# Mixers of a hybrid decoder block: the output transposes and the attention copy take fixed places, and the diagonal products go ahead of the state product

## What is computed

```python
cb = jnp.einsum('bclgn,bcsgn->bcgls', Cc, Bc)
y_diag = jnp.einsum('bcgls,bgjcls,bcsgjp->bclgjp', cb, lmat, X)       # diagonal products
states = jnp.einsum('bclgn,bgjcl,bclgjp->bcgjpn', Bc, decay_states, X)  # state product
h = h * dc[..., None, None] + st                                       # state add, chunk by chunk
y_off = jnp.einsum('bclgn,bcgjpn,bgjcl->bclgjp', Cc, prev, jnp.exp(a_cs))
y = y_diag + y_off + D * xh
y = gated_group_rms_norm(y, z, ssd_norm_w)                             # y * silu(z), normalised per group
probs = softmax with sink over a window of 128 keys; out = probs @ v    # attention
```

## Time and profile before

| | |
|---|---|
| median of 3 runs (lowest to highest) | 2089.53 us (2088.35 to 2092.85) |
| the profiled execution: its time / its span | 2091.65 us / 2090.0 us |
| mean granted TensorE clock | 0.988 of full speed |
| TensorE busy | 2003.9 us, 96% of the span |
| VectorE busy | 1402.8 us, 67% |
| ScalarE busy | 991.1 us, 47% |
| GpSimd busy | 655.4 us, 31% |
| HBM traffic | 122 GB/s over the span |

### The profile page before, as it was taken

How to read it: one execution, slowest core, us unless ns; L and a number is a source line. 1 busy time by engine, 2 the same in 40 slices (tenths; PEclk the granted TensorE clock), 3 DMA queues, 4 the chain that set the end, 5 groups by cost and what they waited for, 6 DMA issues and landing times. The chain is left out here.

```text
span 2090.0 us, 26993 instructions
## 1 busy us (share of the span) xinstructions
PE 2003.9 (96%) x9516; PEld 1618.7 (77%) x9516; DVE 1402.8 (67%) x1892; ACT 991.1 (47%) x1847; POOL 655.4 (31%) x477
## 2 busy tenths in 40 slices
PE   6999999999999898989899999999999999999997
PEld 6787788888866666766578888888888888888886
DVE  6867776865768787878743444569877787753523
ACT  5543344444367666676642223445443444343532
POOL 6524334422365555556400000015222222100000
PEclk9999999999999999999999999999999999999999
DMA  4244324433354444344454443312222222455453
GB/s 156 91 115 138 127 88 152 146 106 114 126 190 132 137 117 148 118 140 117 159 172 168 141 148 125 123 73 85 81 75 90 90 72 78 157 175 189 117 147 92
DMA packets 166092, 261.99 MB, mean 125 GB/s; under 512 B 18400, under 2 KB 108896, under 8 KB 165984
## 3 DMA queue, kind: packets, MB, share of 16 engines
q1 hardware_dynamic: 132016, 217.06, 32.2%
q0 software_dynamic: 8368, 30.94, 4.3%
q10 hardware_dynamic: 25600, 12.59, 2.0%
HBM read 191.73 MB, written 63.57 MB: 122 GB/s over the span
## 5 line engine op out<-in xcount | busy, mean ns | idle before, releaser
L2736 DVE TENSOR_TENSOR lt_d_lo<-lt_w_raw,lt_d_hi 128x640 fp32r<-128x640 f32 (+1 forms) x62 | 55.2, 891 | 133.2 <-ACT lt_d_hi L2435 133.1
L163 PE MATMUL ps_zg<-z_w,u_hi 128*128 128x512 f32 x256 | 110.9, 433 | 0.5 <-POOL z_w L688 0.5
L2306 POOL TENSOR_TENSOR lt_t_f<-lt_w_raw 128x512 f32<-128x512 f32 x21 | 29.1, 1384 | 261.6 <-DVE lt_t_lo L2664 259.8
L994 DVE TENSOR_TENSOR fr_w_lo<-fr_w_f,fr_w_hi 128x512 fp32r<-128x512 f32 x72 | 57.1, 809 | 79.9 <-ACT fr_w_hi L754 61.0
L2435 ACT ACTIVATE lt_d_hi<-lt_w_raw 128x640 fp32r<-128x640 f32 (+1 forms) x62 | 49.1, 792 | 118.5 <-PE lt_ps L165 102.2
L1535 POOL TENSOR_TENSOR mx_seg<-mx_seg,mx_cbm 128x1024 f32<-128x1024 f32 x31 | 75.0, 2418 | 94.1 <-ACT mx_seg L1614 78.5
L165 PE MATMUL ps_zg<-z_w,u_lo 128*128 128x512 f32 x256 | 103.4, 404 | 0.0
L164 PE MATMUL ps_zg<-z_w,u_hi 128*128 128x512 f32 x256 | 102.8, 402 | 0.0
L2393 ACT ACTIVATE lt_t_hi<-lt_t_f 128x512 fp32r<-128x512 f32 x84 | 52.5, 628 | 100.1 <-PE lt_ps L165 61.9
L643 POOL TENSOR_TENSOR fr_w_f<-fr_raw_b 128x512 f32<-128x512 f32 x24 | 36.8, 1534 | 185.3 <-PE fr_ps_x L165 71.0
L2480 ACT ACTIVATE lt_w_hi<-lt_w_raw 128x1024 fp32r<-128x1024 f32 x22 | 23.2, 1060 | 147.4 <-PE lt_ps L165 147.4
(11 more groups left out here) (535 smaller groups left out, 6740.3 us busy)
## 6 DMA issues: line engine op xcount, KB each, us to landing
lt_w_raw<-in_w_up SPq DMA_DIRECT2D x44, 512.0 KB, 4.4
work<-acs_s SPq DMA_DIRECT2D x32, 512.0 KB, 4.1
lt_sig<-gate_s SPq DMA_DIRECT2D x24, 512.0 KB, 3.5
lt_w_raw<-in_w_down SPq DMA_DIRECT2D x32, 384.0 KB, 3.1
ff_s<-lt_fo SPq DMA_DIRECT2D x21, 512.0 KB, 5.1
tok_s<-fr_xt SPq DMA_DIRECT2D x20, 512.0 KB, 3.2
lt_w_raw<-in_w_down SPq DMA_DIRECT2D x32, 320.0 KB, 2.9
gate_s<-fr_xc SPq DMA_DIRECT2D x16, 512.0 KB, 6.6
```

The source lines that it names most:

```text
L163: pe.matmul(dst, s_hi, m_hi, start=first, stop=False, skip_group_check=onto)
L994: dve.tensor_tensor(lo, src, hi.bitcast(F32), ALU.subtract).then_inc(op_lo_done, 1)
L2736: dve.tensor_tensor(down_w(m)[1][:, 0:n], w_raw[:, m % 2, 0:n], down_w(m)[0][:, 0:n].bitcast(F32), ALU.subtract).then_inc(dw_lo_done, 1)
```

## The change

Three things are moved; no instruction comes or goes. On ScalarE the copy L1572 (`attended`) stands ahead of the exponential L1614 in every step, where it stood behind L1580. On TensorE the output transposes stand behind k 2 to 4 of z and directly ahead of L1886, and the diagonal products stand ahead of the state product. At c = 7, which has no next step in its group, k 0 and 1 of the next group's z move from behind the diagonal products to ahead of the output transposes.

```diff
             def outputs(g, c, opening, then=()):
...
                 act.activation(y_t[:, j], ps_y[:].rearrange("p (a n) -> p a n", a=4), ACT.Copy).then_inc(y_out, 1)
-                if not copied:
-                    attended(g, c, opening)
                 for k in then:
                     split_z(g + 1, k)
...
-                    if c == 0 and not opening:
-                        attended(g - 1, NT - 1, False)
+                    if not opening:
+                        attended(*((g, c - 1) if c else (g - 1, NT - 1)), first and c <= 2)
                     if not opening:
                         act.wait_ge(seg_min, n + 1)
                         act.activation(seg[:], seg[:], ACT.Exp).then_inc(decays_done, 1)
...
-            outputs(NG - 1, NT - 1, False, False)
+            attended(NG - 1, NT - 1, False)
+            outputs(NG - 1, NT - 1, False)
...
                     last.then_inc(scored, 1)
+                    ahead(AHEAD if opening else 2, 5)
+                    change = c == NT - 1 and not last_group
+                    if change:
+                        z(g + 1, 0, range(0, 2))
                     if not opening:
                         turn_outputs(*before, first and c == 1)
-                    ahead(AHEAD if opening else 2, 5)
                     if c:
                         pe.wait_ge(state_ready, (NT - 1) * g + c)
                         pe.matmul(ps_e[:], bc_f[:, j, 1], state[:], start=True, stop=True).then_inc(off_done, 1)
+                    pe.wait_ge(mix_ready, n + 1)
+                    pe.wait_ge(xdt_ready, n + 1)
+                    for h in range(HPG):
+                        last = pe.matmul(ps_d[:, h * HD:(h + 1) * HD], seg[:, h], xdt[:, h * HD:(h + 1) * HD], start=True, stop=True)
+                    last.then_inc(diag_done, 1)
                     if c < NT - 1:
                         pe.wait_ge(xdec_ready, (NT - 1) * g + c + 1)
                         if not opening:
                             pe.wait_ge(o_out, n)
                         pe.matmul(ps_f[:], b_tok[:, j], xdec[:], start=True, stop=True).then_inc(state_done, 1)
-                    pe.wait_ge(mix_ready, n + 1)
-                    pe.wait_ge(xdt_ready, n + 1)
-                    for h in range(HPG):
-                        last = pe.matmul(ps_d[:, h * HD:(h + 1) * HD], seg[:, h], xdt[:, h * HD:(h + 1) * HD], start=True, stop=True)
-                    last.then_inc(diag_done, 1)
                     ahead(5, KT)
-                    if c == NT - 1 and not last_group:
-                        z(g + 1, 0, range(KT))
+                    if change:
+                        z(g + 1, 0, range(2, KT))
```

More of the change, by code:

```diff
@@ L1572, in attended, with outputs @@
                 act.activation(o_t[:, c % 2], ps_f[:, 0:2 * P].rearrange("p (a n) -> p a n", a=2), ACT.Copy).then_inc(o_out, 1)
-            def outputs(g, c, opening, copied, then=()):
+            def outputs(g, c, opening, then=()):
                 n, j, before = NT * g + c, c % 2, 16 * (4 * g + c // 2)
@@ L1627, in group @@
                     if not opening:
-                        outputs(g if c else g - 1, (c - 1) % NT, first and c <= 2, c == 0, range(2, 4) if change else ())
+                        outputs(g if c else g - 1, (c - 1) % NT, first and c <= 2, range(2, 4) if change else ())
                     ending = last and c == NT - 1
```

## The result

| | before | changed |
|---|---|---|
| median of 4 runs (lowest to highest) | 2090.14 us (2088.35 to 2092.85) | 2111.29 us (2109.29 to 2116.22) |
| the profiled execution: its time / its span | 2091.65 / 2090.0 us | 2109.29 / 2107.6 us |
| TensorE busy | 2003.9 us, 96% | 2005.4 us, 95% |
| VectorE busy | 1402.8 us, 67% | 1380.4 us, 65% |
| mean granted TensorE clock | 0.988 | 0.99 |

The ratio is 1.0102 (95% interval 1.0087 to 1.0117): the change costs 21.3 us, 18.2 to 24.5. Direction and mechanism were forecast. The time lies inside the range, but only 0.7 us under its upper end of 2112; the forecast itself, +13.9, was too small.

What follows compares the result with a forecast made beforehand. TensorE, busy nearly the whole span, was taken as the bound. Middle steps +17.0, late loads -1.5, group ends -3.6, steps c = 0 +2.5, last group's step 6 -0.5 sum to +13.9: 2103 us, range 2096 to 2112.

Steps and rivals of the forecast that it cites:

- Step (c): Middle steps: diagonal products first, so the later state product delays state add, reciprocal and square; +0.85 us a step, +17.0 over 20.
- (a): ScalarE, middle steps: the copy L1572 ahead of the exponential fits into idle time; taken at 0.
- (b): TensorE, middle steps: output transposes behind three k of z end a wait but lead into another; taken at 0.
- Late loads: Six middle steps where GpSimd's L1511 waited for a DMA: some of their 2.6 us comes back, -1.5 (-2.6 to 0).
- the 0.4 of cover: Middle steps: VectorE's own branch was to end near E+7.1, 0.4 us before the square L1658.
- Group ends: Step c = 7 of three groups: z fills TensorE's wait, VectorE's splits set the pace; -1.2 each, -3.6 us (-6 to +2.6).
- c = 0: Groups' opening steps: same delay through the copy to the state, partly hidden by late loads outside the first group; +0.5 each.
- the first step: c = 0 of the first group: the delay through the copy to the state counts in full, +1.0 us.
- R4: Clock rival: two waits in each middle step drop TensorE to 1.2 GHz, 20 steps +21, 2124 us or above; 3%.
- R1: Faster: the loop feels the diagonal's end if the state product ends before E+1.7; 2074 us, 4%.
- R3: Group boundaries win nothing and every c = 0 pays in full: +23, 2113 us; 7%.
- R2: No change: the attention branch hides most of the lateness, say +0.2 a step; about 2090 us, 7%.

Runs made afterwards that it cites:

- e1: Kernel before with one edit: on TensorE the diagonal products go ahead of the state product; 2113.28 us, ratio 1.0098 to the kernel before.
- e12: Changed kernel with the state product issued twice, same result; 2135.58 us, ratio 1.0204 to the kernel before.
- e6: Kernel before with one edit: the copy L1572 ahead of the exponential on ScalarE; 2089.31 us, ratio 0.9982 to the kernel before.
- e10: Kernel before with the early copy and, at c = 7, two k of the next z ahead of the diagonal products, output transposes unmoved; 2082.29 us, ratio 0.9952.
- e8: e2 with, at c = 7, the next group's two k of z behind the output transposes and L1888 instead of ahead; 2082.08 us, ratio 0.9953.
- e2: Changed kernel with the state product back ahead of the diagonal products, its other moves kept; 2085.96 us, ratio 0.9960 to the kernel before.
- e9: Changed kernel with, at c = 7, the two k of z behind the output transposes and L1888, ahead of the diagonal products; 2115.39 us, ratio 1.0099.
- e7: Changed kernel with the state product behind the probability transposes on TensorE and the state add behind the gate on VectorE; 2100.65 us, ratio 1.0042.
- e11: e8 with ScalarE's two stores behind the scaling of the probabilities instead of ahead of the score exponentials; 2068.28 us, ratio 0.9890 to the kernel before.
- e3: Changed kernel with VectorE's reciprocal ahead of the decay product and the state add; 2120.40 us, ratio 1.0129 to the kernel before.

## Why the prediction was right, and where its sizes were off

- **Step (c), the mechanism, held in every position.** Forecast and measured, in us after E: diagonal products 0.06 and 0.06; reciprocal 3.5 and 3.68; idle of TensorE ahead of the transposes 0.4 and 0.63; idle of VectorE ahead of the state add 1.7 and 1.84, with L1898 as releaser; end of L1772 7.1 and 7.11. e1 shows that this step is the whole loss, and e12 that it passes one to one.
- **Its size was cut too fine.** +0.85 a step, and it was +1.06; over 20 steps that is 4 of the missing 7 us. I gave the state product the 1.02 of L1886 and an end at E+2.89; it took 1.08, ended at E+2.97, and the add began at E+3.08. The transposes took 1.09 instead of 1.03, and the square started at E+7.70 instead of E+7.49, 0.11 ahead of the copy's end (E+7.81) as forecast. The prediction had named +1.05 as a bound, in part for this reason.
- **(a) and (b), taken at 0.** Right for this change, by cover: with the swap in place the copy's gain doesn't show (e1 without it, 14.69; the changed kernel, 14.70). Wrong as a price of the copy itself: 0.18 in a typical step where the state product stands first (e6). For the moved transposes 0 was right (e10 against e8).
- **Late loads, -1.5.** Right in kind. The changed kernel's L1511 waits for a load in 18 steps, not 10, for 51.6 us in all, and still 19 of the 20 middle steps are 14.68 to 14.72: the 0.4 of cover absorbed it. The other is the 15.50 at half clock.
- **Group ends, -3.6 forecast, -0.2 measured: the step that failed.** It said that z in the wait would keep the clock up and that only VectorE's splits would pace the rest. It counted the delay of L1580 as 0.8 and left out that z's own wait for its split (2.01) stands ahead of the transposes, and that matmuls behind such a wait can run at 1.2 GHz, as they did in two of three groups. e8 against e2 and e10 against e6 show that z in its better place is worth 7.5 and 5.5 us there; in the changed kernel it was 4.1 (e9).
- **c = 0, +1.5 forecast, -0.5 measured; the first step, +1.0 and +2.2.** At c = 0 the later copy of the state was hidden altogether: in groups 1 to 3 L1511 starts 3.74 to 3.96 after E where it came at 4.46 to 4.98, since its loads land earlier relative to E. In the first step the diagonal products took 2.58 behind an idle of 2.60, not the 2.00 of the earlier trace rows.
- **Luck in the total.** Middle steps, group ends and the first step were forecast 8.2 us too low together, and c = 0 was 2.0 too high. The two errors cancel in part. Had c = 0 cost what was forecast, the measured time would have been 2113, outside the range.
- **R4 was not empty.** The blanket form, every step at half clock, didn't happen: all middle steps but one ran at 1.00. But I took 1.19 of idle in the earlier trace rows as proof that such waits are harmless, and at c = 1 waits just above it were followed by half clock in 10 of 17 cases. The Trainium skill, page "TensorE: Matmul & The Clock Gate", section "A second HAM failure mode: psum-queue depth-cycling", tells of frequent small idle stretches between groups of matmuls that make the clock swing between its levels. The trace agrees that waits between groups of matmuls can bring the clock down (1.34 us, then 0.50 in the step of 15.50). It does not bear the page out for the other middle steps, whose several short waits kept 1.00.
- **R1 to R3.** R1 fell at its stated point: the state product ended at E+2.97, not before E+1.7. R2 fell with the step's +1.06. R3 named the right part, group ends that win nothing, and put the time at 2113, nearer to the 2111 measured than the forecast's 2103; but it had c = 0 pay in full, and outside the first group that cost nothing.

## What to carry to other kernels

Before moving a producer later on one engine, look at what stands behind its consumer in the other engine's queue. The softmax reciprocal had nothing to do with the state product, but stood behind the add that needs it. Putting the producer later still (e7) was no cure either, since it pushed back its own engine's queue. Work that depends on nothing late belongs ahead of a wait; but a filler that has a wait of its own must not stand ahead of something that others wait for. And look for DMA issues in the queue of an engine that computes: taking two stores from ahead of the score exponentials gained 0.6% (about 13 us, e11 against e8), more than the 0.5% that all other moves together gained over the kernel before.

## What the runs showed of the hardware

- A VectorE instruction with two operands in SBUF stretches when it meets GpSimd at work: 0.69 alone, 2.31 when begun 0.14 into a GpSimd product of 1.90, ending 0.55 after it (e3). Instructions of the same size with one operand in PSUM kept their 0.69 in the same stretch. The Trainium skill, page "GPSIMD Engine Reference", section "Specifications", says that GpSimd shares its SBUF interfaces with VectorE and names instructions with two SBUF inputs; this trace agrees, and adds the price.
- Issuing the two stores took ScalarE 0.37 and 0.52 us, in which the score exponentials behind them did not start (e2).
- TensorE's clock fell to 0.50 for some microseconds in the middle of the stage, behind single waits of 1.30 to 1.90 us in 10 of 17 places and behind 1.13 in two more, and stayed at 1.00 behind others of the same length. The first step's diagonal products took 2.00 in three kernels (before, e6, e11), 2.58 to 2.86 in six (2.58 in the changed one) and 3.67 in e1, e3, e7, e8 and e9. In these five, and in e2 and e10 (2.65 and 2.75), the clock had fallen before: it stood at 0.50 to 0.53 over the 3 us ahead of E already. So the wait just ahead, 0.24 us only in e8, doesn't explain the first step.
